# Gathering tokens for four experts at once from two fp32r parts, in the expert loop of a two-layer decoder trunk

## The reference

```
routed = sum over e in top8(token) of gate[token, e] * ((silu(x @ w1[e]) * (x @ w3[e])) @ w2[e])
```

## Time and profile before

| | |
|---|---|
| median of three runs | 1616.43 us (1613.86 to 1617.93) |
| span of the profiled execution, first to last instruction | 1614.1 us |
| instructions in it | 27930 |
| TensorE busy | 1536.1 us, 95% |
| VectorE busy | 525.0 us, 33% |
| ScalarE busy | 336.6 us, 21% |
| GpSimd busy | 63.6 us, 4% |
| moved by DMA | 461.22 MB, mean 286 GB/s |

### The profile page before, as it was taken

How to read it: one execution, slowest core, us unless ns; L and a number is a source line. 1 busy time by engine, 2 the same in 40 slices (tenths; PEclk the granted TensorE clock), 3 DMA queues, 4 the chain that set the end, 5 groups by cost and what they waited for, 6 DMA issues and landing times.

```text
span 1614.1 us, 27930 instructions
## 1 busy us (share of the span) xinstructions
PE 1536.1 (95%) x11392; PEld 1007.6 (62%) x11392; DVE 525.0 (33%) x1023; ACT 336.6 (21%) x750; POOL 63.6 (4%) x83
## 2 busy tenths in 40 slices
PE   4978899999999999999899988999999999999997
PEld 2466576666666666666478575766666666666653
DVE  0276351323222232222510235232222322223234
ACT  0125222121211212112210231222112221112211
POOL 2030040000000000000000004000000000000000
PEclk9977999999999999999999999999999999999999
DMA  9430049998999999897554504599899898998941
GB/s 294 138 157 1 1 180 385 381 384 362 384 371 375 384 364 385 365 379 291 177 185 154 208 1 157 231 384 385 363 384 384 361 384 363 385 380 365 384 162 52
DMA packets 80748, 461.22 MB, mean 286 GB/s; under 512 B 9152, under 2 KB 9376, under 8 KB 30528
## 3 DMA queue, kind: packets, MB, share of 16 engines
q1 hardware_dynamic: 78112, 452.07, 70.4%
q0 software_dynamic: 2592, 8.53, 1.8%
HBM read 459.52 MB, written 1.05 MB: 285 GB/s over the span
## 4 chain that ended last, share of the span: by engine, by line
PE 90%; DVE 5%; ACT 2%; DMA 1%; issue 1%; SPq 0%; DVEq 0%
PE ps L867 28%; PE ps L894 14%; PE ps L838 13%; PE ps L908 8%; PE ps L998 4%; PE ps L595 4%; PE ps L754 3%; PE ps L709 3%; PE ps L726 2%; PE ps L778 1%; DMA ring<-in_ev_w_in_dram 1%; PE ps L850 1%; PE ps L853 1%; PE ps L567 1%; PE ps L876 1%; ACT roped L1021 1%
## 5 line engine op out<-in xcount | busy, mean ns | idle before, releaser
L867 PE MATMUL ps<-ring,proj 128*64 128x256 f32 x4096 | 456.2, 381 | 1.4 <-ACT proj L1159 1.4
L867 PEld LDWEIGHTS ps<-ring,proj 128*64 128x64 f32 x4096 | 291.1, 137 | 159.1 <-issue 23.0
L1594 DVE TENSOR_TENSOR o_tok<-ps,o_tok 128x1024 f32<-128x1024 f32 x128 | 156.7, 1224 | 422.9 <-PE ps L908 422.9
L894 PE MATMUL ps<-ring,proj 128*64 128x512 f32 x1024 | 233.8, 598 | 0.0
L838 PEld LDWEIGHTS ps<-sel_bf,x_part 128*128 128x128 bf16 x3072 | 200.7, 148 | 41.4 <-issue 41.4
L838 PE MATMUL ps<-sel_bf,x_part 128*128 128x128 bf16 x3072 | 217.1, 227 | 0.0
L1586 DVE SCALAR_TENSOR_TENSOR roped<-roped,rows,ps 128x256 f32<-128x256 f32 x64 | 30.8, 481 | 344.2 <-ACT roped L1166 344.2
L894 PEld LDWEIGHTS ps<-ring,proj 128*64 128x64 f32 x1024 | 67.8, 136 | 114.5 <-issue 110.4
L1192 ACT ACTIVATE y_hi<-ps 128x1024 fp32r<-128x1024 f32 x64 | 65.5, 1023 | 274.8 <-PE ps L908 269.7
L908 PE MATMUL ps<-y_hi,selT 128*128 128x512 f32 x256 | 112.5, 439 | 4.0 <-DVE y_lo L1600 4.0
L908 PE MATMUL ps<-y_lo,selT 128*128 128x512 f32 x256 | 102.7, 401 | 0.0
(11 more groups left out here) (236 smaller groups left out, 1268.7 us busy)
## 6 DMA issues: line engine op xcount, KB each, us to landing
ring<-in_exp_w_dram SPq DMA_DIRECT2D x384, 1024.0 KB, 8.7
ring<-in_od_w_in_dram SPq DMA_DIRECT2D x6, 2048.0 KB, 8.7
ring<-in_ev_w_in_dram SPq DMA_DIRECT2D x4, 2048.0 KB, 27.0
ring<-in_ple_w_gate_dram SPq DMA_DIRECT2D x4, 2048.0 KB, 10.9
ring<-in_sh_w_dram SPq DMA_DIRECT2D x6, 1024.0 KB, 7.0
ring<-in_ev_w_o_dram SPq DMA_DIRECT2D x2, 2048.0 KB, 9.2
ring<-in_od_w_o_dram SPq DMA_DIRECT2D x2, 2048.0 KB, 9.5
gb_row<-in_ln_g_dram POOLq DMA_DIRECT2D x4, 512.0 KB, 4.0
```

Source lines behind the costliest of these rows:

```text
L867: ins = pe.matmul(ps[b * SLOTS:(b + 1) * SLOTS, 2, w * FE:(w + 1) * FE], xe[:, par, c, b * SLOTS:(b + 1) * SLOTS], views[b][w][:, c, :], s ...
L894: ins = pe.matmul(ps[b * SLOTS:(b + 1) * SLOTS, 4 + half, :], hT[:, f, b * SLOTS:(b + 1) * SLOTS], views[b][:, f, half * PIECE:(half + 1) ...
L1594: dve.tensor_tensor(y_acc[:, t, :], ps[:, bank:bank + 2, :].rearrange("p b n -> p (b n)"), y_acc[:, t, :], ALU.add)\
```

## The change

x is split into two fp32r parts (`x_hi`, `x_lo`) instead of three bf16 ones, by one copy and one subtraction a token tile on GpSimd instead of five operations. The one-hot of the gather is now built for four experts (256 slots) at once, in fp32r and in bf16, so that VectorE's build comes once every two pairs with 256 elements an operation. The gather of a quad is 8 chunks x 2 tiles x 2 parts = 32 multiplies of 256 columns. It is issued in two halves of 16: the even step of a pair issues the half for chunks 0 to 3, the odd step the half for chunks 4 to 7, and both are placed between exp_up(m) and h_transpose(m). Both halves write PSUM banks 0 and 1, so each half has its own `xe_copy` and waits for the copy of the half before. The second half no longer stands between scatter and exp_down. Nothing is gathered in the last two steps of a layer.

The one-hot transpose reads the bf16 one-hot against a bf16 identity (cast once, at the start) and writes bf16 into PSUM. The gates are split into three bf16 parts (`split_gates`, four VectorE operations a layer), and the gate pick multiplies the bf16 one-hot with all three, six columns; ScalarE adds the three with `accum_out`. The loop bodies hold four steps in place of two. SP's loads and their waits are as before.

```diff
-                for t in range(NT):
-                    pool.wait_ge(sem(f"ln1_out{L}"), t + 1)
-                    rest = x_tok[:, t, :]
-                    for part in (x_part1, x_part2):
-                        step(pool.tensor_copy(part[:, t, :], rest))
-                        step(pool.tensor_tensor(x_rest, rest, part[:, t, :], ALU.subtract))
-                        rest = x_rest
-                    pool.tensor_copy(x_part3[:, t, :], rest).then_inc(sem("x_split"), 1)
+                    step(pool.tensor_copy(x_hi[:, t, :], x_tok[:, t, :]))
+                    pool.tensor_tensor(x_lo[:, t, :], x_tok[:, t, :], x_hi[:, t, :], ALU.subtract).then_inc(sem("x_split"), 1)
...
-                def gather(m, par, half):
+                def gather(q, qpar, half):
                     if half == 0:
-                        pe.wait_ge(sem("sel_built"), m + (M0 + 1))
-                        if M0 or not isinstance(m, int) or m > 0:
-                            pe.wait_ge(sem("xe_copied"), m + M0)
-                    for c in range(4 * half, 4 * half + 4):
+                        pe.wait_ge(sem("sel_built"), q + (Q0 + 1))
+                    if Q0 or not isinstance(q, int) or 2 * q + half > 0:
+                        pe.wait_ge(sem("xe_copied"), 2 * q + (2 * Q0 + half))
+                    for c in range(4):
                         for t in range(NT):
-                            for part in x_parts:
-                                ins = pe.matmul(ps[:, c // 4, (c % 4) * P:(c % 4 + 1) * P], part[:, t, c::DC],
-                                                sel_bf[:, par, t, :], start=(t == 0 and part is x_part1),
-                                                stop=(t == NT - 1 and part is x_part3))
+                            for part in (x_hi, x_lo):
+                                ins = pe.matmul(ps[:, c // 2, (c % 2) * QSLOT:(c % 2 + 1) * QSLOT],
+                                                part[:, t, 4 * half + c::DC], sel[:, qpar, t, :],
+                                                start=(t == 0 and part is x_hi), stop=(t == NT - 1 and part is x_lo))
...
                     for t in range(NT):
-                        pe.transpose(ps[:, 3, t * P:(t + 1) * P], sel[:, par, t, :], ident)
+                        pe.transpose(ps[:, 3, t * HD:(t + 1) * HD].bitcast(BF16), sel_bf[:, u // 2, t, own], ident_bf)
                     for t in range(NT):
-                        ins = pe.matmul(ps[:, 3, SEQ:SEQ + 2], sel[:, par, t, :], gates[:, t, cols],
+                        ins = pe.matmul(ps[:, 3, SEQ:SEQ + 6], sel_bf[:, u // 2, t, own], gates_bf[:, t, :, cols],
                                         start=(t == 0), stop=(t == NT - 1))
...
-                    exp_up(m, u, first and M0 == 0)
+                    exp_up(m, u, par, first and M0 == 0)
                     if gather_next:
-                        gather(m + 1, 1 - u, 0)
+                        gather(q + 1, 1 - u // 2, par)
                     h_transpose(m)
                     if scatter_last:
-                        scatter(m - 1, 0, 1 - u, M0 == 0 and isinstance(m, int) and m == 1)
-                    if gather_next:
-                        gather(m + 1, 1 - u, 1)
-                    exp_down(m, u, first and M0 == 0)
-                    if gather_next:
-                        sel_transpose(m + 1, 1 - u)
+                        scatter(m - 1, 0, 1 - par, M0 == 0 and isinstance(m, int) and m == 1)
+                    exp_down(m, par, first and M0 == 0)
+                    if selT_next:
+                        sel_transpose(m + 1, (u + 1) % 4)
...
-                    if build:
-                        sel_build(m + 2, u)
+                    if build and u % 2:
+                        q = m // 2 if isinstance(m, int) else (m - 1) // 2
+                        sel_build(q + 2, u // 2)
```

More of the change, by code:

```diff
@@ L52 @@
 PAIRS = NE // 2
+QUADS = NE // 4
+QSLOT = 4 * SLOTS
 RING = 4
@@ L187, in build_trunk @@
         slot_gate = rows[:, 492:494]
+        gate_parts = rows[:, 494:497]
+        gate_rest = rows[:, 136:136 + NT * NE].rearrange("p (t e) -> p t e", t=NT)
         chosen = roped[:, 1, 0:128].rearrange("p (t n) -> p t n", t=NT)
@@ L847, in sel_transpose @@
+                    ins.then_inc(sem("gathered"), 1)
+                def sel_transpose(m, u, first=False):
+                    pe.wait_ge(sem("sel_built"), m // 2 + (Q0 + 1) if isinstance(m, int) else (m - u % 2) // 2 + (Q0 + 1))
                     if not first:
                         pe.wait_ge(sem("hT_copied"), m + M0)
+                    own = slice((u % 2) * P, (u % 2) * P + P)
                     for t in range(NT):
-                        pe.transpose(ps[:, 3, t * P:(t + 1) * P], sel[:, par, t, :], ident)
+                        pe.transpose(ps[:, 3, t * HD:(t + 1) * HD].bitcast(BF16), sel_bf[:, u // 2, t, own], ident_bf)
@@ L851, in sel_transpose, with exp_up @@
                     for t in range(NT):
                         cols = slice(2 * m, 2 * m + 2) if isinstance(m, int) else bass.ds(2 * m, 2)
-                        ins = pe.matmul(ps[:, 3, SEQ:SEQ + 2], sel[:, par, t, :], gates[:, t, cols],
+                        ins = pe.matmul(ps[:, 3, SEQ:SEQ + 6], sel_bf[:, u // 2, t, own], gates_bf[:, t, :, cols],
                                         start=(t == 0), stop=(t == NT - 1))
                     ins.then_inc(sem("selT_tp"), 1)
-                def exp_up(m, par, first):
-                    pe.wait_ge(sem("xe_copied"), m + (M0 + 1))
+                def exp_up(m, u, par, first):
+                    if isinstance(m, int):
+                        pe.wait_ge(sem("xe_copied"), 2 * (m // 2) + (2 * Q0 + 2))
+                    else:
+                        pe.wait_ge(sem("xe_copied"), m + (2 * Q0 + 2 - u % 2))
@@ L911, in scatter, with pe_step @@
                     ins.then_inc(sem("scattered"), 1)
-                def pe_step(m, u, gather_next=True, scatter_last=True, first=False):
+                def pe_step(m, u, gather_next=True, selT_next=True, scatter_last=True, first=False):
+                    par = u % 2
                     for b in range(2):
-                        k = ks + 1 + 2 * u + b
+                        k = ks + 1 + 2 * par + b
                         if isinstance(m, int):
@@ L940, in _ @@
                 pe.wait_ge(sem("shared_added"), NT * L + 2)
+                pe.wait_ge(sem("ident_cast"), 1)
+                pe.wait_ge(sem("gates_split"), L + 1)
                 sel_transpose(0, 0, first=True)
                 pe_step(0, 0, scatter_last=False, first=True)
[L943 to L948, removed]
+                for u in range(1, 4):
+                    pe_step(u, u)
+                with pe.Fori(1, PAIRS // 4 - 1) as i:
+                    for u in range(4):
+                        pe_step(4 * i + u, u)
+                for u in range(4):
+                    pe_step(PAIRS - 4 + u, u, gather_next=u < 2, selT_next=u < 3)
                 pe.wait_ge(sem("over_flag"), L + 1)
@@ L1152, in later, with xe_copy @@
                     return M0 > 0 or not isinstance(m, int) or m >= n
[L1154 to L1160, removed]
+                Q0 = L * QUADS
+                def xe_copy(q, qpar, half):
+                    act.wait_ge(sem("gathered"), 2 * q + (2 * Q0 + half + 1))
+                    if later(q, 2):
+                        act.wait_ge(sem("exp_up"), 2 * q + (M0 - 2))
+                    act.activation(xe[:, qpar, 4 * half:4 * half + 4, :], ps[:, 0:2, :].rearrange("p b (c n) -> p (b c) n", c=2),
+                                   ACT.Copy).then_inc(sem("xe_copied"), 1)
                 def silu(m):
@@ L1192, in y_high, with act_step @@
                     act.activation(y_hi[:, :], ps[:, 4:6, :], ACT.Copy).then_inc(sem("y_high"), 1)
-                def act_step(m, u, more=True):
+                def act_step(m, u, gather_next=True, selT_next=True):
                     silu(m)
                     hT_copy(m)
-                    if more:
-                        xe_copy(m + 1, 1 - u)
+                    if gather_next:
+                        q = m // 2 if isinstance(m, int) else (m - u % 2) // 2
+                        xe_copy(q + 1, 1 - u // 2, u % 2)
                     y_high(m)
-                    if more:
-                        selT_copy(m + 1, 1 - u)
-                xe_copy(0, 0)
+                    if selT_next:
+                        selT_copy(m + 1, 1 - u % 2)
+                xe_copy(0, 0, 0)
+                xe_copy(0, 0, 1)
                 selT_copy(0, 0)
[L1205 to L1210, removed]
+                for u in range(4):
+                    act_step(u, u)
+                with act.Fori(1, PAIRS // 4 - 1) as i:
+                    for u in range(4):
+                        act_step(4 * i + u, u)
+                for u in range(3):
+                    act_step(PAIRS - 4 + u, u, gather_next=u < 2)
                 act.wait_ge(sem("over_flag"), L + 1)
```

(11 more changed lines are left out.)

70 lines of the change are left out of this document (41 added, 29 removed).

## The result

The changed kernel takes 1646.68 us (median of 4 runs, 1645.72 to 1648.82) against 1616.16 us before; the ratio is 1.019, 95% interval 1.018 to 1.021. The forecast was 1538 us, faster. It is wrong in sign.

A forecast was written before the change was run, and what follows sets the result against it. TensorE was taken to bound the kernel. Per layer, gather with borders -32.7 us, transpose and pick -9.3, ends +2.95, together -39.1; twice, -78.1 from the 1614.1 us span gives 1536, forecast 1538 us, range 1503 to 1568.

The forecast's parts named there:

- What bounds the kernel: In the expert loops TensorE sets the pace; SP's loads wait for exp_up to free ring slots, 467.5 us.
- The gather multiply, 124 ns: Each 256-column fp32r gather multiply costs 124 ns, making the gather 1.98 us a step in place of 3.17.
- load and multiply in turn: Rival: in the gather the fp32r load is not hidden behind its multiply, 230 ns each, 1647 us; chance 8%.
- Borders, 0.16 us a step: Two more changes from fp32r to float32, gather to h_transpose and scatter to exp_down, cost 0.16 us a step.
- Transpose and pick, 0.34 us: One-hot transpose and gate pick become four bf16 instructions, 0.34 us a step in place of 0.64, saving 0.30.
- Covers: Before h_transpose and exp_down, other TensorE work still hides the waits for gate_h and hT_copy; costed at nothing.
- VectorE: Four one-hot builds of 256 elements every second step, 2.3 us in odd steps, stay hidden.
- DMA costed at nothing: Expert loads need 15.0 us a pair at about 420 GB/s against a 15.44 us step; the ring absorbs differences.
- Ends of the loop: Per layer, first gather +1.2 us, exp_down in step 0 +0.75, step 30 without gather cover +1.0; together +2.95.

The follow-up runs named there:

- e4: The changed kernel with the gather in plain float32 straight from x_tok, one part, step of eight: 1646.90 us.
- e1: The changed kernel with x_hi and x_lo stored chunk by chunk, so that a gather multiply's weights lie side by side: 1520.56 us, 0.941 of the kernel before.
- e2: The changed kernel with every gather multiply cut to 128 moving columns, weights strided as they are: 1666.21 us, one run.
- e3: The changed kernel with gather weights four elements (16 bytes) apart in place of eight: 1638.26 us.
- e5: The changed kernel with gather weights two elements (8 bytes) apart in place of eight: 1520.57 us.
- e8: The changed kernel with only the one-hot transpose and the gate pick undone, in float32 as before: 1677.73 us, one run.
- e9: The changed kernel with weights side by side and x_hi alone gathered, x_lo left out: 1490.07 us.
- e6: The kernel before with its three bf16 parts stored chunk by chunk, nothing else: 1631.03 us, ratio 1.008.

## Why the prediction was wrong, point by point

**What bounds the kernel**: right. TensorE did before and does after, and SP waits for it.

**The gather multiply, 124 ns: this step failed.** It measured 241 ns. The forecast took the price of a weight load of step eight from the token transposes, "since rows 5 have the same stride and width of weights". e4 shows the error on one tensor: transposes 193 ns, multiplies 337. The row was near in shape and step and far in kind. The forecast set these transposes beside contiguous multiplies and saw 124 against 113 ns; contiguous transposes would have hinted that the step has a price, since the trace of before has their loads at 140 ns against 193:

```profile
L603 PEld LDWEIGHTS ps<-const,roped x32: 138/140/143, 70.7 to 111.5; 128*128 128x128 f32 x32
...
L489 PEld LDWEIGHTS ps<-const,x_tok x96: 185/193/231, 4.4 to 1586.5; 128*128 128x128 f32 x96
```

The term is 512 x 0.117 = 60 us a layer, 120 for both, and e1 takes it out again: 126 us.

The rival "load and multiply in turn" named 230 ns and 1647 us, and the time is 1646.68. That agreement is an accident of numbers: the multiply cost 11 ns more than the rival's 230, 11 us in all, and the other terms came out as much lower. Three observations deny the mechanism: e1 (same type, same columns, 120 ns), e2 (half of the columns, still 241), and the first gather of the changed kernel, where the clock halved and the distance stayed (window, then timeline; below them the same two views for scatter):

```profile
244.80:246.50 1.70, 1.70 (x8) 1.62 (x7) 0.00 (x0) 0.00 (x0) 0.00 (x0) 0.50 1.01 429
...
245.32 0.44 PE L841 MATMUL ps<-sel,x_lo 128*128 128x256 f32 x1
245.56 0.44 PE L841 MATMUL ps<-sel,x_hi 128*128 128x256 f32 x1
...
794.70:797.60 2.90, 2.90 (x8) 2.29 (x7) 1.23 (x1) 0.00 (x0) 0.00 (x0) 0.50 0.97 316
...
795.10 0.63 PE L915 MATMUL ps<-y_hi,selT 128*128 128x512 f32 x1
795.53 0.63 PE L915 MATMUL ps<-y_lo,selT 128*128 128x512 f32 x1
```

At 0.50 of full speed, the 1.2 GHz level, scatter's multiplies of 512 columns start 0.43 us apart (795.10, 795.53, in a window at 0.50) where they take 0.23 at 1.00; 256 columns so take about 213 ns instead of 107. The gather's multiplies still stand 0.24 us apart: columns were not in that distance. What is left is the weight load, and its step alone moves the distance in e1, e3 and e5. With this the rule of the Trainium skill ("TensorE: Matmul & The Clock Gate", Part 3, what overlaps and what doesn't), which the prediction weighed for this rival, disagrees too: by it load and multiply would stand in turn, and e1 has 119 ns.

**Borders, 0.16 us a step**: about the size, in part at another place. Gather to h_transpose is 0.24, the gather's own spacing, so no border. Scatter to exp_down is 431.17 to 432.27, 1.10 against 1.01, so 0.09. And 0.12 stands where the forecast had nothing, from exp_up to the gather: its first two starts are 427.02 and 427.38, 0.36 apart.

**Transpose and pick, 0.34 us**: the sign right, the size too cautious. 0.17 us measured; e8, one run, confirms the part by itself.

**Covers**: right. TensorE has no wait on ScalarE or VectorE in the middle steps, with the second half of the gather gone from ahead of exp_down. **VectorE**: busy 111.86 of the 400 us from 300 to 700, 4.80 a step where it was 4.86, and no wait of TensorE for it in that stretch.

**DMA costed at nothing**: the changed kernel's longer step does not test it (share 0.90). It is right in e1, the version that has the forecast's step. There one step of 15.22 us shows a DMA share of 1.01 at 421 GB/s and TensorE no wait on the experts' weights. The 14.9 us of e9 put the limit only 0.3 us below.

**Ends of the loop**: right in kind. The second half of the first gather waited 1.11 us for the copy (1.2 forecast), exp_down(0) 0.56 (0.75), h_transpose(30) 1.00 (1.0). Missed: the clock. In layer 0 the granted clock was 1.00 in the first gather up to 244.50, through sixteen multiplies 241 ns apart, the wait of 1.11 us and eight more such multiplies, and then fell to 0.50. The first exp_up took 8.86 us (247.92 to 256.78) at a mean of 0.79. In e1 the same two waits stand (1.11 and 1.05 us), the clock stays at 1.00, and that exp_up takes 7.05 (244.40 to 251.45). So the waits alone do not do it; the slow loads belong to it. In layer 1 the clock fell in the second half of the first gather too, and was back before exp_up (1048.08 to 1055.13). The two windows, changed kernel and e1:

```profile
247.90:256.80 8.90, 8.88 (x65) 5.95 (x65) 0.00 (x0) 0.66 (x5) 0.00 (x0) 0.79 0.09 38
...
244.40:251.45 7.05, 7.05 (x64) 5.35 (x64) 0.00 (x0) 0.63 (x5) 0.00 (x0) 1.00 0.73 307
```

**The rest of the sum** is checked by e1, where only the failed term is mended: 1520.6 against the forecast's 1538. Its step is 15.22 us against 15.44: 0.17 less for the transpose and pick, 0.05 less for the gather with its borders. Over 58 steps that is 13 of the 17 us; the other 4 are not assigned, and the runs of e1 spread over 6.

## What to carry to other kernels

Look at the step of the stationary operand in bytes before widening its type: at step eight, bf16 weights hid behind the columns, and four-byte weights doubled the multiply. Store such an operand in the order in which it is loaded, and look where the rearranging runs: with two operations on four-byte elements it was free here, with five on the bf16 parts it cost more than it gave. When a price is read from a near row, ask that the operation is the same, not only the shape; and when a rival's time comes out to the microsecond, test its mechanism all the same.

## What the runs showed of the hardware that was not expected

- Weight loads of 128 four-byte elements for a multiply: 191 to 195 ns in the records at a step of one or two elements, 327 to 338 at four or eight, and 119, 121, 233 and 241 ns between multiplies. Transposes of float32: 141 ns side by side, 193 at a step of eight.
- bf16 weights: 98 ns at a step of one, 145 to 148 at eight, which is 16 bytes as well; four-byte weights 16 bytes apart take 328.
- The distance between multiplies with these slow loads was 0.24 us at a granted clock of 1.00 and of 0.50. After stretches of them the clock fell (first gather of layer 0, e2), where e1 with the same waits held 1.00.
- GpSimd casting 1024 elements a partition with an inner write step of 128 elements: 4754 ns to bf16 (1039 in order), 2027 to fp32r (1036 in order). Beside it a small VectorE instruction took 3.59 us instead of 0.22 (e6).
- Expert weights arrived at 419 to 423 GB/s in 30 us windows, at a DMA share of 1.01 to 1.02 (e9).
